# Gate and up of nine chunks a layer in seven block products where there were eight, for half of the contraction, in a two-layer decoder kernel

## The chip, the cores and the metric

The kernel runs on one core of one Trainium2 chip. The metric is the device time of one execution in microseconds (us), the median of several. The engines are TensorE (PE; its weight loads are PEld), VectorE (DVE), ScalarE (ACT), GpSimd (POOL) and the DMA queue of SyncE (SP).

## The reference

Two decoder layers on 256 tokens of width 2048, all in float32. Each layer normalises, projects, runs three causal mixers side by side and adds their output projection to the residual; all of that stays as it is. Then comes the feed-forward part, which the change touches:

```python
h2 = _rmsnorm(x, ffn_norm[l])                       # (256, 2048)
ff = jax.nn.silu(h2 @ w_gate[l]) * (h2 @ w_up[l])   # w_gate, w_up: (2048, 5632)
x = x + ff @ w_down[l]                              # w_down: (5632, 2048)
```

## The kernel before

A float32 product is made of three matmuls in a reduced float32 format: each operand is split into a rounded part (`_hi`) and a remainder (`_lo`), and hi x hi, hi x lo and lo x hi are added in PSUM. The activations `xt_hi`, `xt_lo` stay in SBUF (16 blocks of 128 rows of the contraction by 256 tokens). The weights stream in units: a unit is 4 blocks of 128 x 512 weights, 1 MB, in two transfers of 512 KB. There are four slots (`stage[s]`), taken in turn. For each unit n, SyncE waits until TensorE is done with unit n - 4 (`used[s]`), and loads it (`load`, L486); ScalarE rounds it into `w_hi[s]` (`round_unit`, L1022); VectorE writes the remainder over the staged weights as `w_lo[s]` (`rest_of_unit`, L1332); TensorE runs 24 matmuls of 512 columns on it (`unit`, L631 to L633: 4 blocks, 2 halves of the tokens, 3 matmuls) and raises `used[s]`. Each engine works strictly through its own list; ScalarE and VectorE prepare unit n + 3 (`LEAD = 3`) in the step in which TensorE runs unit n.

The hidden width 5632 is cut into 11 chunks of 512. A chunk is 8 units of gate and up (`gate_up`: 4 of gate, with the results in banks 0 and 1, then 4 of up, in banks 2 and 3) and 4 units of down (`down`, one per 512 columns of the output), where the down of chunk f - 1 follows the gate and up of chunk f. After the gate ScalarE applies Silu (L1253); after the up VectorE multiplies (L1756) into `act_sb`. In the next chunk, behind its second unit, TensorE transposes `act_sb` in eight small matmuls (`ff_turn`, L591) into banks 6 and 7; ScalarE and VectorE split that into `f_hi` and `f_lo` (L1241, L1741). Each down unit adds into `resid` with two VectorE instructions (L1765), which stand in VectorE's list ahead of the remainder of the unit prepared in the same step. The down units use banks 4/5, 0/1, 4/5, 2/3. Chunks 1 to 9 are a loop on every engine (`Fori(1, FF_CHUNKS - 1)`), one turn of it being 12 units; chunk 0 stands before the loop, chunk 10 (the peel) and the last down after it. `made(quad, n)` counts how often a slot has been filled; `x_added` counts the adds into the residual, and `added(f, n)` waits for the n-th of the down of chunk f.

Of the kernel before, what the change touches and what calls it, by code (L numbers as in the profile page):

```python
# [28 lines left out]
P = 128  # L29
# [40 lines left out]
U_BODY = U_FF + 8  # L70
U_PEEL = U_BODY + BODY * (FF_CHUNKS - 2)
# [125 lines left out]
def bank_rounds():  # L197

    used = {b: 0 for b in (4, 5, 6, 7)}
    of = {}  # L200

    def take(layer, key, banks):
        of[layer, key] = {}
        for b in banks:
            of[layer, key][b] = used[b]
            used[b] += 1

    for layer in range(DEPTH):
# [8 lines left out]
        take(layer, ("ff_turn", 0), [6, 7])  # L217
        for b in (6, 7):
            used[b] += FF_CHUNKS - 1
    return of  # L220
# [37 lines left out]
ACT_LINKS, VEC_LINKS = 9, 65  # L258

LAST_ORDER = [[(t, c) for c in range(4) for t in range(NT)], [(t, c) for t in range(NT) for c in range(4)]]  # L260
LAST_BANK = [{(t, c): (2 * (2, 0, 1, 2)[c] + t, *((-1, 6), (-1, 4), (-1, 8), (0, 2))[c]) for c in range(4) for t in range(NT)},
             {(0, 0): (4, -1, 6), (0, 1): (5, -1, 6), (0, 2): (0, -1, 6), (0, 3): (1, -1, 6),
              (1, 0): (2, -1, 8), (1, 1): (3, -1, 8), (1, 2): (0, 0, 3), (1, 3): (1, 0, 4)}]
# [5 lines left out]
def program(nc, x, positions, w_in, w_q_b, w_kv_b, w_out, w_gate, w_up, w_down, gate_w, gains, rows,  # L269
            final_norm, consts, levels, causal, out):  # L270
    with ExitStack() as ctx:
# [57 lines left out]
        stage_x = arena("stage_x", [P, 4 * NCH], F32, 32 * SEQ)  # L329
        w_lo_x = arena("w_lo_x", [P, 4 * NCH], F32R, 32 * SEQ)  # L330
        w_hi_x = arena("w_hi_x", [P, 4 * NCH], F32R, 40 * SEQ)
# [79 lines left out]
        silu_made, act_made, ft_hi_made = sem("silu_made"), sem("act_made"), sem("ft_hi_made")  # L411
# [28 lines left out]
        def made(quad, n):  # L440

            return quad + 1 - (n % 4 < 2)

# [15 lines left out]
        def _(sp):  # L459
# [33 lines left out]
            for layer in range(DEPTH):  # L493
# [45 lines left out]

                load_gate_up(U_FF, 0, 0)  # L540
                with sp.Fori(1, FF_CHUNKS - 1) as f:
                    load_gate_up(U_BODY, 3 * f - 3, f)
                    load_down(U_BODY + 8, 3 * f - 3, f - 1)
                load_gate_up(U_PEEL, 0, FF_CHUNKS - 1)
# [21 lines left out]
        def _(pe):  # L566
# [4 lines left out]
            for layer in range(DEPTH):  # L571
# [67 lines left out]
                def acc_taken(parity, r):  # L639


                    if r == 0:

                        if layer:
                            need(x_added, X_ADDS, NT * (2 + parity))
                        return
# [266 lines left out]
                def ff_turn(f):  # L913

                    pe.wait_ge(act_made, layer * (FF_CHUNKS * NT) + NT * f + NT)
                    for b in (6, 7):
                        pe.wait_ge(bank_free[b], ROUND[layer, ("ff_turn", 0)][b] + f + 1)
                        for i in range(2):
                            for t in range(NT):
                                j = 2 * (b - 6) + i  # L920
                                mm = transpose(bank[b][:, i * SEQ + t * P:i * SEQ + (t + 1) * P],
                                               act_sb[:, t, j * P:(j + 1) * P])
                        mm.then_inc(bank_full[b], 1)
# [5 lines left out]
                def gate_up(f, n0, turn=0):  # L929
                    for half in range(2):  # L930
                        if n0 == U_FF:
                            acc_taken(half, R_FF)
                        else:
                            pe.wait_ge((silu_made, act_made)[half], layer * (FF_CHUNKS * NT) + NT * f)
                            added(f - 2, 4 + 4 * half)
                        for u in range(4):
                            unit(n0 + 4 * half + u, range(4 * u, 4 * u + 4), half, normed, u == 0, u == 3,
                                 turn=turn, norm="norm2" if n0 == U_FF and half == 0 else None)
                            if n0 == U_FF and half == 0 and u == 0:
                                norm_turn("norm2", range(KT // 4, KT // 2))  # L940
                            if half == 0 and u == 1 and n0 != U_FF:
                                ff_turn(f - 1)

                def down(f, c, n0, turn=0):


                    if c == 0:
                        for b in (6, 7):
                            pe.wait_ge(bank_free[b], ROUND[layer, ("ff_turn", 0)][b] + f + 2)
                        added(f - 1, 6)  # L950
                    elif c == 2:
                        added(f, 2)
                    else:
                        pe.wait_ge(silu_made if c == 1 else act_made, layer * (FF_CHUNKS * NT) + NT * (f + 2))

                    def hidden(k):
                        return f_hi[0], f_lo[0], k

                    unit(n0 + c, range(4), (2, 0, 2, 1)[c], hidden, True, True, turn=turn)

                def last_down(f):


                    for b in (6, 7):
                        pe.wait_ge(bank_free[b], ROUND[layer, ("ff_turn", 0)][b] + f + 2)
                    last = layer == DEPTH - 1
                    for t, c in LAST_ORDER[last]:
# [10 lines left out]
                        acc = bank[b][:, :]  # L978
                        wh = hi[:, :].rearrange("p (k n) -> p k n", n=NCH)
                        wl = lo[:, :].rearrange("p (k n) -> p k n", n=NCH)  # L980
                        for k in range(4):
                            a, b = (x[1][:, k, t * P:(t + 1) * P] for x in (f_hi, f_lo))
                            pe.matmul(acc, a, wh[:, k, :], start=k == 0, stop=False)  # L983
                            pe.matmul(acc, a, wl[:, k, :], start=False, stop=False)  # L984
                            mm = pe.matmul(acc, b, wh[:, k, :], start=False, stop=k == 3)  # L985
                        mm.then_inc(used[s] if t else down_made, 1)
                        if not last and t == 1 and c >= 2:
                            norm_turn("norm1", range(2 * c - 4, 2 * c - 2), layer + 1)

                gate_up(0, U_FF)  # L990
                with pe.Fori(1, FF_CHUNKS - 1) as f:
                    gate_up(f, U_BODY, 3 * f - 3)
                    for c in range(4):
                        down(f - 1, c, U_BODY + 8, 3 * f - 3)
                gate_up(FF_CHUNKS - 1, U_PEEL)
                for c in range(4):
                    down(FF_CHUNKS - 2, c, U_PEEL + 8)
                    if c == 1:
                        ff_turn(FF_CHUNKS - 1)
# [3 lines left out]
        def _(act):  # L1003
# [26 lines left out]
            for layer in range(DEPTH):  # L1030
# [206 lines left out]
                def ff_turn(f, to):  # L1237
                    for b in (6, 7):
                        act.wait_ge(bank_full[b], ROUND[layer, ("ff_turn", 0)][b] + f + 1)
                        dst = f_hi[to][:, 2 * (b - 6):2 * (b - 6) + 2, :].rearrange("p a b -> p (a b)")  # L1240
                        act.activation(dst, bank[b][:, :], ACT.Copy).then_inc(ft_hi_made, 1)  # L1241

                def gate_up(f, n0, turn=0):
                    for i in range(8):
                        round_unit(layer * QUADS + (n0 + i + LEAD) // 4 + turn, n0 + i + LEAD)
                        if i == 1 and n0 != U_FF:
                            ff_turn(f - 1, 0)
                        if i == 3:
                            if n0 == U_FF:
                                need(rstd_made, len(POW), POW["norm2"] + 1)  # L1250
                            act.wait_ge(used[3], layer * QUADS + (n0 + 3) // 4 + 2 + turn)
# [5 lines left out]
                with act.Fori(1, FF_CHUNKS - 1) as f:  # L1257
                    gate_up(f, U_BODY, 3 * f - 3)
                    for c in range(4):
                        n = U_BODY + 8 + c + LEAD  # L1260
                        round_unit(layer * QUADS + n // 4 + 3 * f - 3, n)
                gate_up(FF_CHUNKS - 1, U_PEEL)
                for c in range(4):
                    n = U_PEEL + 8 + c + LEAD
# [3 lines left out]
                    round_unit(layer * QUADS + n // 4, n)  # L1268
                    if c == 1:
                        ff_turn(FF_CHUNKS - 1, 1)  # L1270
# [53 lines left out]
        def _(vec):  # L1324
# [22 lines left out]
            for layer in range(DEPTH):  # L1347
# [388 lines left out]
                def ff_turn(f, to):  # L1736
                    for b in (6, 7):
                        vec.wait_ge(bank_full[b], ROUND[layer, ("ff_turn", 0)][b] + f + 1)
                        vec.wait_ge(ft_hi_made, layer * (2 * FF_CHUNKS) + 2 * f + b - 5)
                        at = slice(2 * (b - 6), 2 * (b - 6) + 2)  # L1740
                        vec.tensor_tensor(f_lo[to][:, at, :].rearrange("p a b -> p (a b)"), bank[b][:, :],  # L1741
                                          f_hi[to][:, at, :].rearrange("p a b -> p (a b)").bitcast(F32), ALU.subtract)\
                           .then_inc(bank_free[b], 1)

                def gate_up(f, n0, turn=0):
                    for i in range(8):
                        rest_of_unit(layer * QUADS + (n0 + i + LEAD) // 4 + turn, n0 + i + LEAD)
                        if i == 1 and n0 != U_FF:
                            ff_turn(f - 1, 0)
                        if i == 7:  # L1750
                            if n0 == U_FF:
                                need(rstd_made, len(POW), POW["norm2"] + 1)
                            vec.wait_ge(used[3], layer * QUADS + (n0 + 7) // 4 + 2 + turn)
# [6 lines left out]
                def down(c, n0, turn=0):  # L1760
                    n = n0 + c
                    vec.wait_ge(used[n % 4], layer * QUADS + n // 4 + 2 + turn)
                    for t in range(NT):
                        part = resid[:, t, c * NCH:(c + 1) * NCH]
                        vec.tensor_tensor(part, bank[2 * (2, 0, 2, 1)[c] + t][:, :], part, ALU.add).then_inc(x_added, 1)  # L1765
                    if n == U_PEEL + 9 and layer == DEPTH - 1:
                        vec.wait_ge(hi_made_x, 1)
                        vec.tensor_tensor(w_lo_x[:, :], stage_x[:, :], w_hi_x[:, :].bitcast(F32), ALU.subtract)\
                           .then_inc(lo_made_x, 1)
                    rest_of_unit(layer * QUADS + (n + LEAD) // 4 + turn, n + LEAD)  # L1770
# [42 lines left out]
                with vec.Fori(1, FF_CHUNKS - 1) as f:  # L1813
                    gate_up(f, U_BODY, 3 * f - 3)
                    for c in range(4):
                        down(c, U_BODY + 8, 3 * f - 3)
                gate_up(FF_CHUNKS - 1, U_PEEL)
                for c in range(4):
                    down(c, U_PEEL + 8)
                    if c == 1:  # L1820
                        ff_turn(FF_CHUNKS - 1, 1)
# [58 lines left out]
```

## Time and profile before

| | |
|---|---|
| median of 3 runs | 2231.94 us (2230.34 to 2232.48) |
| the profiled execution | 2232.38 us |
| its span, first to last instruction | 2230.6 us |
| PE busy | 2212.5 us (99%), 11060 matmuls |
| PEld busy | 1889.3 us (85%) |
| DVE busy | 1277.2 us (57%) |
| ACT busy | 948.6 us (43%) |
| mean granted TensorE clock | 0.998 |
| moved by DMA | 402.67 MB, mean 181 GB/s |

Busy time is the time in which an engine has an instruction in work; matmuls are pipelined, so two of them overlap in the record (each 0.39 us long, one starting every 0.227 us), and their busy time is counted once. The chain that ended last is followed back from the last instruction, at each step to what released it.

### The profile page before, as it was taken

Reading aid. Unit: us, or ns where it says so; the run is one execution under the profiler, and the core shown is the slowest. Engines: PE = TensorE matmul, PEld = TensorE weight load, DVE = VectorE, ACT = ScalarE, POOL = GpSimd, SP = SyncE. Lnnn points to the kernel's source line nnn. Section 1 sums busy time; section 2 is a strip of 40 time slices with the busy share of each in tenths; the row PEclk is TensorE's granted clock in tenths of the full one; section 3 lists DMA queues with packets and bytes.
Section 4 is the critical chain, followed back from the end, with each engine's and each line's share of the span. In section 5 each row is a group of like instructions: output and inputs, shape, how many; then the busy total and the mean of one; then the engine's idle time right before and its main releaser. Section 6 shows DMA issues by size and latency. Waiting matters only on the chain.

```text
span 2230.6 us, 27421 instructions
## 1 busy us (share of the span) xinstructions
PE 2212.5 (99%) x11060; PEld 1889.3 (85%) x11060; DVE 1277.2 (57%) x1372; ACT 948.6 (43%) x964; POOL 24.0 (1%) x24
## 2 busy tenths in 40 slices
PE   9999999999999999999999999999999999999998
PEld 7899988888888888888888999888888888888886
DVE  5576774555455555555655866745555455555555
ACT  5554544533333333333443635444333333333333
POOL 0000000000000000000000000000000000000000
PEclk9999999999999999999999999999999999999999
DMA  7543455555555555555555435555555555555554
GB/s 249 183 134 117 157 170 189 182 191 192 189 188 188 188 190 190 192 190 192 193 179 160 147 114 166 174 171 189 197 190 192 190 189 188 188 190 189 192 191 160
DMA packets 221094, 402.67 MB, mean 181 GB/s; under 512 B 13376, under 2 KB 53600, under 8 KB 220896
## 3 DMA queue, kind: packets, MB, share of 16 engines
q1 hardware_dynamic: 220304, 400.90, 54.9%
q8 instruction: 50, 0.82, 0.1%
q10 hardware_dynamic: 720, 0.78, 0.1%
q14 instruction: 20, 0.16, 0.0%
HBM read 399.54 MB, written 2.10 MB: 180 GB/s over the span
## 4 chain that ended last, share of the span: by engine, by line
PE 97%; DMA 1%; DVE 1%; issue 1%; ACT 0%; SPq 0%; POOLq 0%; POOL 0%; ACTq 0%; DVEq 0%
PE bank L631 29%; PE bank L633 29%; PE bank L632 29%; PE bank L591 2%; DMA stage<-in_w_in 1%; PE bank L756 1%; PE bank L985 0%; PE bank L983 0%; PE bank L984 0%; PE bank L697 0%; PE bank L820 0%; PE bank L808 0%; PE bank L698 0%; PE bank L699 0%; PE bank L707 0%
## 5 line engine op out<-in xcount | busy, mean ns | idle before, releaser
L1332 DVE TENSOR_TENSOR w_lo<-stage,w_hi 128x2048 fp32r<-128x2048 f32 (+4 forms) x397 | 859.3, 2166 | 710.5 <-ACT w_hi L1022 710.4
L1022 ACT ACTIVATE w_hi<-stage 128x2048 fp32r<-128x2048 f32 (+4 forms) x397 | 719.8, 1815 | 957.7 <-DMA stage<-in_w_down 308.7
L631 PE MATMUL bank<-w_hi,xt_hi 128*128 128x512 f32 (+4 forms) x2328 | 876.6, 377 | 6.4 <-DVE xt_lo L1393 4.3
L633 PE MATMUL bank<-w_hi,xt_lo 128*128 128x512 f32 (+4 forms) x2328 | 867.7, 373 | 0.0
L632 PE MATMUL bank<-w_lo,xt_hi 128*128 128x512 f32 (+4 forms) x2328 | 867.0, 372 | 0.0
L631 PEld LDWEIGHTS bank<-w_hi,xt_hi 128*128 128x128 f32 x2328 | 437.7, 188 | 80.0 <-issue 11.8
L633 PEld LDWEIGHTS bank<-w_hi,xt_lo 128*128 128x128 f32 x2328 | 437.5, 188 | 69.0
L632 PEld LDWEIGHTS bank<-w_lo,xt_hi 128*128 128x128 f32 x2328 | 437.9, 188 | 67.8
L631 PE MATMUL bank<-w_hi,f_hi 128*128 128x512 f32 x640 | 249.1, 389 | 0.0
L633 PE MATMUL bank<-w_hi,f_lo 128*128 128x512 f32 x640 | 249.0, 389 | 0.0
L632 PE MATMUL bank<-w_lo,f_hi 128*128 128x512 f32 x640 | 249.0, 389 | 0.0
L1765 DVE TENSOR_TENSOR resid<-bank,resid 128x512 f32<-128x512 f32 x160 | 103.0, 685 | 82.1 <-PE bank L633 81.8
L633 PEld LDWEIGHTS bank<-w_hi,f_lo 128*128 128x128 f32 x640 | 120.1, 188 | 24.9
L632 PEld LDWEIGHTS bank<-w_lo,f_hi 128*128 128x128 f32 x640 | 120.1, 188 | 24.9
L631 PEld LDWEIGHTS bank<-w_hi,f_hi 128*128 128x128 f32 x640 | 120.1, 188 | 24.9
L631 PE MATMUL bank<-w_hi,mix_hi 128*128 128x512 f32 x96 | 38.5, 402 | 0.0
L633 PE MATMUL bank<-w_hi,mix_lo 128*128 128x512 f32 x96 | 37.9, 395 | 0.0
L632 PE MATMUL bank<-w_lo,mix_hi 128*128 128x512 f32 x96 | 37.9, 394 | 0.0
L1200 ACT ACTIVATE e<-e,nmx 128x128 f32<-128x128 f32 x72 | 31.8, 446 | 13.3 <-DVE nmx L1633 13.3
L1067 ACT ACTIVATE xt_hi<-bank,gain_sb 128x256 fp32r<-128x256 f32 x64 | 24.9, 480 | 24.3 <-PE bank L591 23.6
L1393 DVE SCALAR_TENSOR_TENSOR xt_lo<-bank,gain_sb,xt_hi 128x256 fp32r<-128x256 f32 x64 | 26.4, 476 | 14.2 <-ACT xt_hi L1067 13.9
L1206 ACT ACTIVATE pt<-bank 128x384 f32<-128x384 f32 x24 | 11.8, 490 | 50.6 <-PE bank L591 50.6
(213 smaller groups left out, 1231.9 us busy)
## 6 DMA issues: line engine op xcount, KB each, us to landing
stage<-in_w_gate SPq DMA_DIRECT2D x176, 512.0 KB, 4.3
stage<-in_w_up SPq DMA_DIRECT2D x176, 512.0 KB, 4.4
stage<-in_w_down SPq DMA_DIRECT2D x174, 512.0 KB, 4.4
stage<-in_w_in SPq DMA_DIRECT2D x96, 384.0 KB, 3.7
stage<-in_w_out SPq DMA_DIRECT2D x64, 512.0 KB, 4.4
stage<-in_w_in SPq DMA_DIRECT2D x54, 512.0 KB, 4.6
stage<-in_w_in SPq DMA_DIRECT2D x16, 320.0 KB, 3.4
stage<-in_w_q_b SPq DMA_DIRECT2D x12, 384.0 KB, 3.6
```

What stands on the lines that cost most here:

```text
L591: return pe.transpose(dst, src, ident)
L631: pe.matmul(acc, a, wh[:, i, :], start=first and i == 0, stop=False)
L632: pe.matmul(acc, a, wl[:, i, :], start=False, stop=False)
L633: mm = pe.matmul(acc, b, wh[:, i, :], start=False, stop=last and i == len(kts) - 1)
L756: done[par] = pe.matmul(dst, k[rows_, g, t * P:(t + 1) * P], moving, start=True, stop=True)
L1022: act.activation(w_hi[s][:, 0:kts * cols], stage[s][:, 0:kts * cols], ACT.Copy).then_inc(hi_made[s], 1)
L1067: act.activation(xt_hi[:, kt, :], bank[b][:, i * SEQ:(i + 1) * SEQ], ACT.Copy, scale=gain_sb[:, at, g0 + kt:g0 + kt + 1]).then_inc(xt_hi_m ...
L1200: last = act.activation(part, part, ACT.Exp, bias=nmx[:, k:k + 1], scale=scale, accum_out=esum[:, k:k + 1])
L1206: act.activation(pt[PT_OF[j]][:, :], ps[:, 0:3 * P], ACT.Copy).then_inc(bank_free[4], 1)
L1332: vec.tensor_tensor(w_lo[s][:, 0:kts * cols], stage[s][:, 0:kts * cols], w_hi[s][:, 0:kts * cols].bitcast(F32), ALU.subtract).then_inc(lo_ ...
L1393: ins = vec.scalar_tensor_tensor(xt_lo[:, kt, :], bank[b][:, i * SEQ:(i + 1) * SEQ], gain_sb[:, at, g0 + kt:g0 + kt + 1], xt_hi[:, kt, :]. ...
L1765: vec.tensor_tensor(part, bank[2 * (2, 0, 2, 1)[c] + t][:, :], part, ALU.add).then_inc(x_added, 1)
```

## The change

Chunks 0 and 1 of a layer stay as they were. For chunks 2 to 10 the first 8 of the 16 blocks of the contraction are computed as 2 x 2 block products in the manner of Strassen and Winograd: the two halves of the tokens by two halves of these 8 blocks, times two halves of the contraction by gate and up. Four set units (the even ones of a chunk's eight) hold one block of each of the four kinds: two of gate, two of up. TensorE makes 7 products of such a unit (`set_unit`), each into a bank of its own, where a unit had 8. The four odd units (`pair_unit`) hold two blocks of gate and two of up of the other half of the contraction, 8 products as before. What the seven products need is made as follows.

- Of the weights, VectorE makes four sums per set unit (three instructions; the second sum is written over the unit's last block) ahead of the remainders, and ScalarE rounds them: three blocks at once, then, when the sums are there, the fourth and the three others.
- Of the activations, `mixed_tokens` makes four mixed blocks once a layer, in chunk 0.
- The seven results are brought together by `combine` (four VectorE adds behind U+6, with one copy by ScalarE) and `activate` (four VectorE adds behind U+7, then the multiplications, with the Silus on ScalarE in between).

With all eight banks taken by a set chunk, the banks of down become 4/6, 5/7, 4/6, 5/7, the transposes of chunk f go behind the down of chunk f - 1, and in VectorE's list the adds into the residual move one step later, behind the preparation of the unit of the step before. The diff, cut to its core:

```diff
+SET_CHUNKS = FF_CHUNKS - FIRST_SET          # FIRST_SET = 2
+DOWN_BANKS = (4, 6), (5, 7), (4, 6), (5, 7)
+TURN_BANKS = (4, 6), (0, 1)
...
+        def in_set(n):
+            return U_BODY <= n < U_LAST and (n - U_BODY) % BODY < 8 and n % 2 == 0
...  # TensorE
+                def set_unit(n, q, f, turn):
+                    s = n % 4
+                    pe.wait_ge(lo_made[s], made(layer * QUADS + n // 4, n) + turn)
...
+                    if q == 0:
+                        pe.wait_ge(act_made, layer * (FF_CHUNKS * NT) + NT * f)
+                        pe.wait_ge(xs_made, layer + 1)
+                    product(0, token(0, q), raw[0], q == 0, False)
+                    product(1, mixed_x[3], raw[2], q == 0, False)
+                    product(2, token(1, q), summed[2], q == 0, False)
+                    if q == 0:
+                        added(f - 2, 8)
+                    product(7, mixed_x[0], summed[1], q == 0, q == 3)
+                    product(5, mixed_x[2], summed[0], q == 0, q == 3)
+                    if q == 0:
+                        hidden_in(f - 1)
+                    product(4, token(0, q + 4), raw[1], q == 0, q == 3)
+                    product(6, mixed_x[1], raw[3], q == 0, q == 3).then_inc(used[s], 1)
...
+                def down(f, c, n0, turn=0, after_set=True):
                     if c == 0:
+                        hidden_in(f)
+                        if after_set:
+                            pe.wait_ge(first_kept, layer * SET_CHUNKS + f + 2 - FIRST_SET)
+                            pe.wait_ge(combined, layer * (2 * SET_CHUNKS) + 2 * (f + 1 - FIRST_SET) + 1)
+                    elif c == 1:
+                        if after_set:
+                            pe.wait_ge(combined, layer * (2 * SET_CHUNKS) + 2 * (f + 1 - FIRST_SET) + 2)
                     else:
+                        added(f, 2 * c - 2)
...
+                with pe.Fori(FIRST_SET, FF_CHUNKS - 1) as f:
+                    gate_up_sets(f, U_BODY, 3 * f - 3 * FIRST_SET)
+                    for c in range(4):
+                        down(f - 1, c, U_BODY + 8, 3 * f - 3 * FIRST_SET)
+                    added(f - 1, 6)
+                    ff_turn(f, TURN_BANKS[0])
...  # ScalarE, prepare(n) of a set unit
+                    act.wait_ge(full[s], made(quad, n) * 32)
+                    act.activation(w_hi[s][:, 0:3 * NCH], stage[s][:, 0:3 * NCH], ACT.Copy).then_inc(raw_hi_made, 1)
+                    if between:
+                        between()
+                    act.wait_ge(sums_made, layer * (4 * SET_CHUNKS) + set_index(n) + 1 + sets)
+                    act.activation(w_hi[s][:, 3 * NCH:], stage[s][:, 3 * NCH:], ACT.Copy)
+                    act.activation(sums_hi[s // 2][:, :, :], sums[s // 2][:, :, :], ACT.Copy).then_inc(hi_made[s], 1)
...  # VectorE, prepare(n) of a set unit
+                    vec.wait_ge(full[s], made(quad, n) * 32)
+                    vec.tensor_tensor(x[:, 0:2, :], w[:, 1:3, :], w[:, 3:4, :].to_broadcast([P, 2, NCH]), ALU.add)\
+                       .then_inc(sum_chain, 1)
+                    vec.wait_ge(sum_chain, 2 * k + 1)
+                    vec.tensor_tensor(w[:, 3, :], x[:, 0, :], w[:, 2, :], ALU.add).then_inc(sum_chain, 1)
+                    vec.wait_ge(sum_chain, 2 * k + 2)
+                    vec.tensor_tensor(x[:, 2, :], w[:, 3, :], w[:, 0, :], ALU.add).then_inc(sums_made, 1)
+                    if between:
+                        between()
...
+                    vec.tensor_tensor(w_lo[s][:, 0:3 * NCH], stage[s][:, 0:3 * NCH], w_hi[s][:, 0:3 * NCH].bitcast(F32),
+                                      ALU.subtract)
+                    vec.wait_ge(hi_made[s], made(quad, n))
+                    vec.tensor_tensor(w_lo[s][:, 3 * NCH:], stage[s][:, 3 * NCH:], w_hi[s][:, 3 * NCH:].bitcast(F32),
+                                      ALU.subtract)
+                    vec.tensor_tensor(sums_lo[s // 2][:, :, :], x[:, :, :], sums_hi[s // 2][:, :, :].bitcast(F32),
+                                      ALU.subtract).then_inc(lo_made[s], 1)
...
+                def down(f, n0, turn=0, sets=0, after_set=True):
+                    def between():
+                        add_down(3, n0, turn)
+                        ff_turn(f + 1, TURN_BANKS[0], 0)
+                    for c in range(4):
+                        if c == 0 and after_set:
+                            activate(f + 1, n0 - 8, turn)
+                        if c:
+                            add_down(c - 1, n0, turn)
+                        prepare(n0 + c + LEAD, turn, sets, between if c == 3 else None)
```

## Rows read from the trace of the kernel before

**Rows 1.** The page: busy time of each engine, and the chain that ended last, by engine.

```profile
PE 2212.5 (99%) x11060; PEld 1889.3 (85%) x11060; DVE 1277.2 (57%) x1372; ACT 948.6 (43%) x964; POOL 24.0 (1%) x24
...
PE 97%; DMA 1%; DVE 1%; issue 1%; ACT 0%; SPq 0%; POOLq 0%; POOL 0%; ACTq 0%; DVEq 0%
```

**Rows 2.** One loop turn: the window's row; then a piece of the chain (start, us, what).

```profile
607.99:674.16 66.17, 66.17 (x297) 54.86 (x296) 35.09 (x24) 25.13 (x16) 0.00 (x0) 1.00 0.57 190
...
641.28 0.88 PE bank L591 x8
```

**Rows 3.** Timeline of PE at U+8: start, us, engine, line, what.

```profile
608.24 0.39 PE L633 MATMUL bank<-w_hi,xt_lo 128*128 128x512 f32 x1
...
608.92 0.39 PE L633 MATMUL bank<-w_hi,f_lo 128*128 128x512 f32 x1
```

**Rows 4.** Timeline: a unit's last matmul and its slot's next rounding (middle: U+7, ended 608.63).

```profile
481.30 0.39 PE L633 MATMUL bank<-w_hi,f_lo 128*128 128x512 f32 x1
...
487.57 1.92 ACT L1022 ACTIVATE w_hi<-stage 128x2048 fp32r<-128x2048 f32 x1 [3.91 <-DMA stage<-in_w_gate]
...
613.92 1.92 ACT L1022 ACTIVATE w_hi<-stage 128x2048 fp32r<-128x2048 f32 x1 [3.37 <-DMA stage<-in_w_down]
...
707.09 0.39 PE L633 MATMUL bank<-w_hi,xt_lo 128*128 128x512 f32 x1
...
712.46 1.92 ACT L1022 ACTIVATE w_hi<-stage 128x2048 fp32r<-128x2048 f32 x1 [2.43 <-DMA stage<-in_w_up]
```

**Rows 5.** VectorE by shape, whole span: what, xcount | busy us, mean ns | idle before.

```profile
L1332 DVE TENSOR_TENSOR w_lo<-stage,w_hi 128x2048 fp32r<-128x2048 f32 x321 | 735.3, 2292 | 661.2 <-ACT w_hi L1022 661.2
L1765 DVE TENSOR_TENSOR resid<-bank,resid 128x512 f32<-128x512 f32 x160 | 103.0, 685 | 82.1 <-PE bank L633 81.8
L1332 DVE TENSOR_TENSOR w_lo<-stage,w_hi 128x1536 fp32r<-128x1536 f32 x54 | 94.7, 1753 | 28.2 <-ACT w_hi L1022 28.2
L1756 DVE SCALAR_TENSOR_TENSOR act_sb<-bank,rstd_x,act_sb 128x512 f32<-128x512 f32 x44 | 30.9, 743 | 0.0
...
L1332 DVE TENSOR_TENSOR w_lo<-stage,w_hi 128x1024 fp32r<-128x1024 f32 x6 | 7.3, 1222 | 2.8 <-ACT w_hi L1022 2.7
```

**Rows 6.** ScalarE by shape, whole span.

```profile
L1022 ACT ACTIVATE w_hi<-stage 128x2048 fp32r<-128x2048 f32 x321 | 615.0, 1917 | 943.9 <-DMA stage<-in_w_down 308.7 <-DMA stage<-in_w_gate 288.6 <-DMA stage<-in_w_up 266.2
L1022 ACT ACTIVATE w_hi<-stage 128x1536 fp32r<-128x1536 f32 x54 | 79.8, 1478 | 2.4 <-DMA stage<-in_w_in 2.2
L1253 ACT ACTIVATE act_sb<-bank,rstd_x 128x512 f32<-128x512 f32 x44 | 27.4, 674 | 0.0
...
L1028 ACT ACTIVATE w_hi<-stage 128x512 fp32r<-128x512 f32 x4 | 2.4, 634 | 3.5 <-DMA stage<-in_w_in 3.5
```

**Rows 7.** Timeline of VectorE from the remainder prepared at U+7 to the adds of c0.

```profile
610.58 2.29 DVE L1332 TENSOR_TENSOR w_lo<-stage,w_hi 128x2048 fp32r<-128x2048 f32 x1 [3.37 <-ACT w_hi L1022]
612.79 1.40 DVE L1756 SCALAR_TENSOR_TENSOR act_sb<-bank,rstd_x,act_sb 128x512 f32<-128x512 f32 x2
614.11 1.28 DVE L1765 TENSOR_TENSOR resid<-bank,resid 128x512 f32<-128x512 f32 x2
```

**Rows 8.** Chain at a restart of TensorE, in layer 1's projection.

```profile
1210.05 1.93 ACT w_hi L1022
...
1212.00 2.30 DVE w_lo L1332
1214.30 0.14 issue
1214.43 0.36 PE bank L631
```

**Rows 9.** Start of the kernel: first matmul after a pause; the window behind it.

```profile
17.74 0.77 PE L631 MATMUL bank<-w_hi,xt_hi 128*128 128x512 f32 x1 [2.95 <-DVE xt_lo L1393]
...
17.70:20.40 2.70, 2.66 (x6) 2.15 (x7) 1.90 (x3) 2.61 (x5) 0.00 (x0) 0.50 1.05 387
```

**Rows 10.** VectorE instruction that waits for its own last result.

```profile
L1586 DVE TENSOR_TENSOR p<-p,row_sb 128x512 f32<-128x512 f32 x4 | 2.8, 692 | 0.1
```

More of the change, by code:

```diff
@@ L941, in gate_up @@
                             if half == 0 and u == 1 and n0 != U_FF:
-                                ff_turn(f - 1)
-                def down(f, c, n0, turn=0):
-                    if c == 0:
[L948 to L952, printed above, removed]
-                    else:
[L954 to L959, printed above, removed]
+                                ff_turn(f - 1, TURN_BANKS[0])
@@ new lines, in pair_unit @@
+                def pair_unit(n, m, turn):
+                    s = n % 4
+                    pe.wait_ge(lo_made[s], made(layer * QUADS + n // 4, n) + turn)
+                    for i in range(2):
+                        for t in range(NT):
+                            for part in range(2):
+                                b = 2 * part + i
+                                mm = product(2 * t + part, token(t, 8 + 2 * m + i),
+                                             (blocks(w_hi[s])[:, b, :], blocks(w_lo[s])[:, b, :]),
+                                             2 * t + part == 3 and m + i == 0, m == 3 and i == 1)
+                    mm.then_inc(used[s], 1)
@@ L1734, in _, with ff_turn @@
                 norm2()
[L1736 to L1740, printed above, removed]
+                def ff_turn(f, banks, to):
+                    for half, b in enumerate(banks):
+                        vec.wait_ge(turned, layer * (2 * FF_CHUNKS) + 2 * f + half + 1)
+                        vec.wait_ge(ft_hi_made, layer * (2 * FF_CHUNKS) + 2 * f + half + 1)
+                        at = slice(2 * half, 2 * half + 2)
@@ L1764, in down @@
                         part = resid[:, t, c * NCH:(c + 1) * NCH]
[L1765 to L1770, printed above, removed]
+                        vec.tensor_tensor(part, bank[DOWN_BANKS[c][t]][:, :], part, ALU.add).then_inc(x_added, 1)
+                def down(f, n0, turn=0, sets=0, after_set=True):
+                    def between():
+                        add_down(3, n0, turn)
+                        ff_turn(f + 1, TURN_BANKS[0], 0)
+                    for c in range(4):
+                        if c == 0 and after_set:
+                            activate(f + 1, n0 - 8, turn)
+                        if c:
+                            add_down(c - 1, n0, turn)
+                        prepare(n0 + c + LEAD, turn, sets, between if c == 3 else None)
                 def add_last(t, c):
@@ L1812, in _ @@
                 gate_up(0, U_FF)
[L1813 to L1817, printed above, removed]
-                for c in range(4):
-                    down(c, U_PEEL + 8)
-                    if c == 1:
-                        ff_turn(FF_CHUNKS - 1, 1)
+                gate_up(1, U_SECOND)
+                down(0, U_SECOND + 8, after_set=False)
+                with vec.Fori(FIRST_SET, FF_CHUNKS - 1) as f:
+                    gate_up_sets(f, U_BODY, 3 * f - 3 * FIRST_SET, 4 * f - 4 * FIRST_SET)
+                    down(f - 1, U_BODY + 8, 3 * f - 3 * FIRST_SET, 4 * f - 4 * FIRST_SET)
+                gate_up_sets(FF_CHUNKS - 1, U_PEEL)
+                for c in range(4):
+                    if c == 0:
+                        activate(FF_CHUNKS - 1, U_PEEL, 0)
+                    else:
+                        add_down(c - 1, U_PEEL + 8)
+                    if c == 1 and layer == DEPTH - 1:
+                        vec.wait_ge(hi_made_x, 1)
+                        vec.tensor_tensor(w_lo_x[:, :], stage_x[:, :], w_hi_x[:, :].bitcast(F32), ALU.subtract)\
+                           .then_inc(lo_made_x, 1)
+                    if c == 2:
+                        ff_turn(FF_CHUNKS - 1, TURN_BANKS[1], 1)
+                    prepare(U_PEEL + 8 + c + LEAD)
+                add_down(3, U_PEEL + 8)
+                vec.wait_ge(x_added, layer * X_ADDS + X_ADDS)
                 assert count[0] == VEC_LINKS, count[0]
```

254 lines of the change are left out of this document (191 added, 63 removed).

## The prediction, made before the change was run

> **What bounds the kernel now.** The busy line comes first: TensorE 99%, VectorE 57% of the span. The chain that ended last says the same from the other side, 97% of it TensorE [rows 1]. The time is thus matmuls times their spacing, and everything else counts only where TensorE comes to wait. Next, one turn of the feed-forward loop by window and by chain: 66.17 us, TensorE busy for all of it, at the full granted clock, VectorE for 35.09 us, ScalarE for 25.13 us, and eight transposes of 0.88 us [rows 2]. Last, single instructions: three matmuls start every 0.68 us, so one product (three matmuls of 512 columns) is 0.68 us and a unit of eight products 5.44 us [rows 3]. Twelve units are 65.28 us, and with the transposes 66.16: there is no wait in a turn.
>
> **What goes.** A chunk's gate and up have 64 products before. After, four set units have 7 each and four pair units 8 each: 60. So 4 x 0.68 = 2.72 us go per set chunk, with nine set chunks a layer and two layers 18 x 2.72 = 49.0 us. Every matmul keeps its form (128x128 against 512 columns), so I keep its spacing. Bytes and DMA sizes are as before: a unit is still two transfers of 512 KB, in rows of 512 numbers.
>
> **What comes, by engine.** A set unit costs VectorE one add of 1024 columns, two of 512, then remainders of 1536, 512 and 1536: 1.222 + 2 x 0.685 + 2 x 1.753 + 0.685 = 6.78 us, less about 0.2 where one starts before the last has ended, where it was 2.29 [rows 5]. Per chunk VectorE has 4 x 6.6 (sets) + 8 x 2.29 (pair and down units) + four adds of combining, four of activating, eight into the residual and two remainders of the turn, 18 x 0.64, and two multiplications, 1.4: 58 us. ScalarE has 4 x (1.478 + 0.634 + 1.478) + 8 x 1.917 + about 3.5 = 33 us [rows 6]. The new turn has 63.4 us of TensorE. No engine is over its share, but VectorE goes from 53% to 91% of a turn, in strict order, and so its order has to be walked.
>
> **The walk.** Let U be a chunk's first unit, c0 to c3 its four down units, and t = 0 the end of U+7, just before c0. I use: an end counts when the record has it, 0.16 us after the next matmul could start (0.39 long, 0.227 apart [rows 3]); the data of a slot are there 5.25 us after the end of the unit that used it, a case near the middle is 5.29, the shortest found 4.98, the longest 5.88 [rows 4]; VectorE's next instruction starts 0.09 us before the last ends where nothing holds it [rows 7] and 0.02 behind it where it needs its result [rows 10]; another engine's result is taken up 0.02 to 0.04 us later [rows 8], and TensorE's first matmul starts 0.13 us behind what it waited for [rows 8].
>
> 1. U+6 ends at -5.44. Its slot takes U+10 (c2), whose data are there at -0.2. VectorE is in the remainder of U+9 until -0.7, then starts combining; the first difference, which frees banks 4 and 6, is ready at -0.14. c0 starts at 0.0 in place of -0.16: wait 0.16 us.
> 2. Combining ends at 1.75, the remainder of U+10 at 4.03. Only then comes `activate`, behind it in order: four adds, 3.94 to 6.4; ScalarE's two Silus run 4.7 to 5.9, and the two multiplications end at 7.8.
> 3. U+11 (c3): data at 5.25, ScalarE, held by the Silus, 5.84 to 7.76; remainder 7.79 to 10.08.
> 4. Only now the adds of c0 (c0 had ended at 5.60): to 11.27. c2 uses c0's banks and could start at 10.88, starts at 11.40: wait 0.52 us.
> 5. U+12, the next chunk's first set unit: data at 5.60 + 5.25 = 10.85. Sums 11.18 to 13.84; ScalarE's second part 13.88 to 15.90; VectorE's first remainder to 15.63, then it stands for ScalarE, then 15.93 to 18.28.
> 6. Only now the adds of c1 (c1 had ended at 11.04): 18.19 to 19.46. c3 uses banks 5 and 7, as c1 did, and waits for just these (`added(f, 4)`). c2's last matmul has made room at 16.84; c3 starts at 19.59: wait 2.75 us.
> 7. Behind it: remainder of U+13 to 21.7, adds of c2 to 22.9, sums of U+14 to 25.4, adds of c3 to 26.6, remainders of the turn to 28.1. TensorE ends c3 at 25.0, turns until 25.9, and reaches the wait for c3's adds at 27.9 and that for the turn's remainders at 29.3: 1.2 us to spare at both. U+14 is ready at 31.9 and wanted at 36.1, and inside the eight units the slack only grows.
>
> So a loop turn waits 0.16 + 0.52 + 2.75 = 3.43 us and saves 2.72: 63.44 + 3.43 = 66.87 us where it was 66.17. The kernel before had the same adds, but ahead of the remainder in each step and beside ordinary remainders of 2.29 us: there each step's adds follow their unit's end at once [rows 7].
>
> **Sum.** Per layer, nine set chunks save 24.5. Eight loop turns wait 27.4; the down of chunk 0, before the loop, already prepares U+12 as a set unit, but has no `activate`: 0.07 + 2.85 = 2.9; the last chunk's down prepares ordinary units: only the 0.16 ahead of c0. Together 30.5: a layer is 6.0 us longer, two 12.1. Arrival is not even, and only late data add to the wait while early ones are cut short by other waits: I add 1. The mixed tokens, in chunk 0, are one operation of 2048, four of 512 and one of 2048, 7.3 us a layer; units there have 3.1 us of VectorE idle each, and 6.8 us between being ready and being wanted, of which 5 are used by the longest piece: nothing. Without this cover they would cost 7 a layer. The tail behind the last down is unchanged. The profiled execution took 2232.4 (span 2230.6), so 2245.5; the median is 0.4 less: 2245.
>
> **Bounds of what no row shows.** Each of these moves the wait before c3 one for one, so 18 times. The 1024 add takes one of its sources by broadcast: as a 512 one or as a 1536 one, 0.69 or 1.75 in place of 1.22, so -10 or +10 us; I take 1.22, the width that it writes [rows 5]. Arrival: 5.0 to 5.9 against 5.25, -4 or +12. A wait on its own result: 0.0 to 0.1 us, two per chain: up to +3. A start without the overlap of 0.09, where the many waits between VectorE's instructions would break it: some ten of them from `activate` to c1's adds, not all on the chain: up to +20. TensorE's restart, 0.13 us in its one row: 0 to 0.3, -2 or +3. The forecast's own range is 2229 to 2262.
>
> **Rivals.**
> (a) *The clock falls in the wait.* After 2.95 us without a matmul at the start of the kernel the granted clock was 0.50, that is 1.2 of 2.4 GHz, for 2.7 us, six matmuls 0.45 us apart in place of 0.227: 1.34 us lost [rows 9]. The wait before c3 is 2.75 to 2.9 us, nearly as long. If each of the 18 does this: 24 us more, 2269. Against it: this wait is a little shorter, and it is the only such row. The Trainium skill, "TensorE: Matmul & The Clock Gate", section "Why this matters for your kernels", asks for no idle stretches between bursts of matmuls, as one lets the engine fall to half rate; the trace agrees once, at 2.95 us, and no row of this case has a wait of 2.75.
> (b) *The wait isn't there* (the other side). It needs the adds of c1 to be done by 16.7, that is 2.75 us of step 2 to 6 to be gone: VectorE would take c1's adds ahead of the remainders of U+12, or TensorE's wait would be met by earlier adds. By the written order neither is so: for c2 and c3 `added(f, 2 * c - 2)` asks for 2 and 4, and `add_down(1)` stands behind `prepare` of U+12. If only the short waits stay: 49.0 - 18 x 0.68 = 37 gained, 2195. It decides from the point at which the chain from c0's end to c1's adds is under 11.1 us; I have 13.9.
> (c) *VectorE is the bound throughout.* Its 52 instructions a chunk carry more waits than before. With 0.1 us more on each, 5.2 us a turn, half of it lies on the path: about +33 over the forecast, 2278. For it: 91% busy already in the sum. Against: waits between engines cost 0.02 to 0.04 us in every row of before.
> (d) *A shorter chain*: same waits, but each link at its low bound (-14 in all): 2231, no change.
>
> **Chances.** Forecast 0.58, (a) 0.15, (b) 0.12, (c) 0.06, (d) 0.09. Within 0.2% of the time before (about what a measurement here can tell from no change) is 2227.5 to 2236.4. Faster: (b), and a part of (d): 0.16. Same: the rest of (d) and the low end of the forecast: 0.14. Slower: 0.70. The range 2226 to 2270 leaves out (b) and (c).
>
> **What would show it.** In the profile after, one loop turn lasts 66.9 us and its TensorE is busy for some 63.4. The longest wait of TensorE is by the adds into the residual, once a turn, 2.7 us, 18 in all (nine a layer); behind it 0.5 us by the same line, and 0.16 by combining. VectorE's last remainder of U+12 ends right before the adds of c1. No wait inside the eight gate and up units. A granted clock below 1.00 in the loop, with matmuls 0.45 us apart behind the long wait, speaks for (a); loop turns of 63.4 to 64.2 us for (b); waits of TensorE for weight remainders for (c). I would be wrong altogether if a matmul's spacing were to change, or if waits stood inside gate and up.

## The result, and the profile after

The changed kernel takes 2268.81 us (median of 4, 2266.61 to 2272.14) where the kernel before takes 2231.26: a ratio of 1.0169, 95% interval 1.0152 to 1.0187. It is slower, as forecast (2245), and by 37.5 us in place of 13 to 14. The number is that of rival (a), 2269, in which the clock falls in the wait before c3.

The page of the changed kernel, against [rows 1]: VectorE went from 1277 to 1684 us, TensorE from 11060 to 10844 matmuls, that is 18 x 12 fewer, and the chain that ended last is no longer TensorE almost alone.

```profile
PE 2195.1 (97%) x10844; PEld 1856.5 (82%) x10844; DVE 1684.0 (74%) x1888; ACT 1076.8 (48%) x1128; POOL 24.0 (1%) x24
...
PE 75%; DVE 10%; issue 6%; DMA 5%; ACT 3%; SPq 1%; DVEq 0%; POOLq 0%; POOL 0%; ACTq 0%
```

The waits of TensorE (engine, line waited for: us, times, longest): one pair of lines that the kernel before doesn't have leads, matmuls of down behind the adds into the residual.

```profile
PE bank L994 <- DVE resid L1997: 50.8, 34, 2.9
```

Two loop turns by window (us, PE busy, PEld, DVE, ACT, POOL, granted clock, DMA share, GB/s), each from the start of one c3 to the next, against the 66.17 us of [rows 2]. The second is 1.57 us longer and its clock lower; the two last windows show where: the first 3.66 us of each turn hold 16 matmuls in the first and 9 in the second, at a mean granted clock of 0.56.

```profile
630.42:697.57 67.15, 64.30 (x284) 52.39 (x284) 56.97 (x53) 32.05 (x25) 0.00 (x0) 1.00 0.57 188
697.57:766.29 68.72, 65.86 (x284) 53.54 (x284) 57.07 (x53) 32.04 (x25) 0.00 (x0) 0.98 0.56 182
697.57:701.23 3.66, 3.66 (x9) 2.84 (x10) 3.66 (x4) 0.69 (x1) 0.00 (x0) 0.56 0.60 229
630.42:634.08 3.66, 3.66 (x16) 3.04 (x17) 3.66 (x4) 0.84 (x1) 0.00 (x0) 1.00 0.60 231
```

The timeline of TensorE at the start of the second window (start, us, engine, line, what). c3's first matmul starts 2.79 us behind the start of the one before it, where 0.227 is the usual spacing [rows 3], so it is 2.57 us late. From 698.25 on matmuls start 0.43 us apart, as at 1.2 GHz (half clock, in what follows), and the spacing comes back behind 701.57.

```profile
694.78 0.39 PE L996 MATMUL bank<-w_hi,f_lo 128*128 128x512 f32 x1
697.57 0.50 PE L994 MATMUL bank<-w_hi,f_hi 128*128 128x512 f32 x1 [2.40 <-DVE resid L1997]
697.91 0.53 PE L995 MATMUL bank<-w_lo,f_hi 128*128 128x512 f32 x1
698.25 0.63 PE L996 MATMUL bank<-w_hi,f_lo 128*128 128x512 f32 x1
698.67 0.63 PE L994 MATMUL bank<-w_hi,f_hi 128*128 128x512 f32 x1
...
701.23 0.49 PE L994 MATMUL bank<-w_hi,f_hi 128*128 128x512 f32 x1
701.57 0.40 PE L995 MATMUL bank<-w_lo,f_hi 128*128 128x512 f32 x1
```

All 18 waits before c3 are there: 16 of 2.56 to 2.58 us, and the first of each layer with 3.02 and 2.81. Behind 11 of the 18 six to eight matmuls follow 0.43 us apart; the longest wait, 3.02 us, is not among the 11.

VectorE's own timeline, up to the c3 at 630.42, can be laid beside the walk of the prediction. Its t = 0, the end of U+7, is 610.64 here. The walk had the sums of U+12 from 11.18, the last remainder to 18.28, c1's adds from 18.19 and c3 at 19.59; the rows have 11.42, 18.52, 18.44 and (630.42) 19.78.

```profile
614.72 0.68 DVE L1976 TENSOR_TENSOR kept<-bank,kept 128x512 f32<-128x512 f32 x1
...
618.66 2.28 DVE L1481 TENSOR_TENSOR w_lo<-stage,w_hi 128x2048 fp32r<-128x2048 f32 x1
620.86 1.28 DVE L1997 TENSOR_TENSOR resid<-bank,resid 128x512 f32<-128x512 f32 x2
622.06 1.21 DVE L1905 TENSOR_TENSOR sums<-stage 128x1024 f32<-128x1024 f32 x1
623.30 0.69 DVE L1908 TENSOR_TENSOR stage<-sums,stage 128x512 f32<-128x512 f32 x1
624.03 0.69 DVE L1910 TENSOR_TENSOR sums<-stage 128x512 f32<-128x512 f32 x1
624.75 1.76 DVE L1915 TENSOR_TENSOR w_lo<-stage,w_hi 128x1536 fp32r<-128x1536 f32 x1
626.80 0.69 DVE L1918 TENSOR_TENSOR w_lo<-stage,w_hi 128x512 fp32r<-128x512 f32 x1 [0.29 <-ACT sums_hi L1365]
627.41 1.75 DVE L1920 TENSOR_TENSOR sums_lo<-sums,sums_hi 128x1536 fp32r<-128x1536 f32 x1
629.08 1.28 DVE L1997 TENSOR_TENSOR resid<-bank,resid 128x512 f32<-128x512 f32 x2
```

### The profile page after: what moved, and what is told of

The parts are those of the page before. It is cut to its first block, busy times and chain, and to the rows that moved or that the text cites. A ratio compares the mean times of both kernels' runs of the same rounds, so it can differ in the third digit from the quotient of the medians.

```text
span 2264.8 us, 27939 instructions
## 1 busy us (share of the span) xinstructions
PE 2195.1 (97%) x10844; PEld 1856.5 (82%) x10844; DVE 1684.0 (74%) x1888; ACT 1076.8 (48%) x1128; POOL 24.0 (1%) x24
## 4 chain that ended last, share of the span: by engine, by line
PE 75%; DVE 10%; issue 6%; DMA 5%; ACT 3%; SPq 1%; DVEq 0%; POOLq 0%; POOL 0%; ACTq 0%
PE bank L994 12%; PE bank L996 11%; PE bank L995 11%; PE bank L673 11%; PE bank L675 11%; PE bank L674 11%; DMA stage<-in_w_down 3%; PE bank L633 2%; ACT w_hi L1130 2%; DVE resid L1997 1%; DVE sums_lo L1920 1%; ACT sums_hi L1365 1%; DVE sums L1905 1%; DMA stage<-in_w_in 1%; DVE w_lo L1481 1%
## 5 line engine op out<-in xcount | busy, mean ns | idle before, releaser
L1481 DVE TENSOR_TENSOR w_lo<-stage,w_hi 128x2048 fp32r<-128x2048 f32 (+3 forms) x325 | 693.8, 2137 | 350.2 <-ACT w_hi L1130 348.8
L1130 ACT ACTIVATE w_hi<-stage 128x2048 fp32r<-128x2048 f32 (+3 forms) x325 | 581.4, 1791 | 434.4 <-DMA stage<-in_w_down 207.5
L673 PE MATMUL bank<-w_hi,xt_hi 128*128 128x512 f32 (+4 forms) x1176 | 426.0, 362 | 4.3 <-DVE xt_lo L1542 3.1
L675 PE MATMUL bank<-w_hi,xt_lo 128*128 128x512 f32 (+4 forms) x1176 | 418.8, 356 | 0.0
L674 PE MATMUL bank<-w_lo,xt_hi 128*128 128x512 f32 (+4 forms) x1176 | 418.4, 356 | 0.0
L994 PE MATMUL bank<-w_hi,xt_hi 128*128 128x512 f32 x720 | 281.6, 391 | 0.0
L996 PE MATMUL bank<-w_hi,xt_lo 128*128 128x512 f32 x720 | 280.2, 389 | 0.0
L995 PE MATMUL bank<-w_lo,xt_hi 128*128 128x512 f32 x720 | 280.1, 389 | 0.0
L1360 ACT ACTIVATE w_hi<-stage 128x1536 fp32r<-128x1536 f32 x72 | 107.3, 1491 | 249.9 <-DMA stage<-in_w_up 249.9
L1915 DVE TENSOR_TENSOR w_lo<-stage,w_hi 128x1536 fp32r<-128x1536 f32 x72 | 126.4, 1755 | 1.8
```

The costliest lines, as they stand in the source:

```text
L673: pe.matmul(acc, a, wh[:, i, :], start=first and i == 0, stop=False)
L674: pe.matmul(acc, a, wl[:, i, :], start=False, stop=False)
L675: mm = pe.matmul(acc, b, wh[:, i, :], start=False, stop=last and i == len(kts) - 1)
L994: pe.matmul(bank[b][:, :], x[0], w[0], start=start, stop=False)
L995: pe.matmul(bank[b][:, :], x[0], w[1], start=False, stop=False)
L996: return pe.matmul(bank[b][:, :], x[1], w[0], start=False, stop=stop)
```

## The experiments

The theory: the order of VectorE's list makes the waits, above all the one before c3, and TensorE's standing still there brings the half clock. Against it stand VectorE's load (57 of 67 us a turn), and a cause of the half clock other than the wait.

**1. c1's adds before the remainders of U+12.** In VectorE's `down`:

```diff
-                        if c:
+                        if c in (1, 3):
                             add_down(c - 1, n0, turn)
-                        prepare(n0 + c + LEAD, turn, sets, between if c == 3 else None)
+                        prepare(n0 + c + LEAD, turn, sets,
+                                {1: lambda: add_down(1, n0, turn), 3: between}.get(c))
```

> The changed kernel with one thing moved in VectorE's list: the adds of c1 into the residual stand between the sums and the remainders of U+12 instead of behind them. Theory (the order of VectorE's list makes the long wait, and the wait makes the clock fall): the wait before c3 (2.57 us a turn) is gone, c2's of about 0.6 us and the 0.2 us before c0 stay, no matmul in the loop runs 0.43 us apart; 18 x 2.6 us of waiting and some 11 x 1.6 us of half clock go from 2268.8: 2203 us. Rival (VectorE's load of 85% is what holds TensorE): the wait moves to another place, remainders of the weights among them, and the time stays above 2230 us.

Measured: 2223.15 us (2220.13 to 2223.43), ratio to the kernel before 0.9958 (0.9941 to 0.9974). The wait before c3 and every half clock of the feed-forward part are gone, the time is under 2230 as the theory has it, but 20 us over its number. The trace of this kernel says where they went: TensorE, earlier now, runs into the wait for c3's adds at the fourth product of the next chunk.

```profile
633.92 0.39 PE L996 MATMUL bank<-sums_hi,xt_lo 128*128 128x512 f32 x1
635.03 0.50 PE L994 MATMUL bank<-sums_hi,xs_hi 128*128 128x512 f32 x1 [0.72 <-DVE resid L1997]
```

It comes 0.88 us late there, and 0.70 to 1.05 us in all 18 places, 14.3 us together; with the slower restart behind each (see below) that is some 16 of the 20 us. The reason stands in VectorE's list of the same kernel: the adds of c3 wait behind the sums of U+14.

```profile
629.74 1.29 DVE L1997 TENSOR_TENSOR resid<-bank,resid 128x512 f32<-128x512 f32 x2
631.11 1.23 DVE L1905 TENSOR_TENSOR sums<-stage 128x1024 f32<-128x1024 f32 x1
632.37 0.69 DVE L1908 TENSOR_TENSOR stage<-sums,stage 128x512 f32<-128x512 f32 x1
633.09 0.69 DVE L1910 TENSOR_TENSOR sums<-stage 128x512 f32<-128x512 f32 x1
633.70 1.28 DVE L1997 TENSOR_TENSOR resid<-bank,resid 128x512 f32<-128x512 f32 x2
```

The 1.2 us to spare of the walk's step 7 were 1.2 us behind a wait of 2.75; take the wait away, and TensorE reaches the wait for c3's adds before they are done. I had not carried that into the expectation.

**2. c0's adds ahead of the remainder of U+11 too.** As in 1, with `if c in (0, 3): add_down(c and c - 1, n0, turn)`.

> As the one before, and the adds of c0 stand ahead of the remainder of U+11 as well, in the step of c0. Theory: the wait of 0.6 us before c2 goes too, with its restart; only the 0.2 us before c0 stays: 2203 - 18 x 0.65 = 2191 us, under both the kernel before and the changed one. Rival (VectorE's load): U+11 or U+12 comes late instead, TensorE waits for a remainder before c3 or before the next chunk, and nothing is gained over the kernel with only c1's adds moved (2203 us).

Measured: 2218.26 us (2217.80 to 2219.81), ratio 0.9942 (0.9925 to 0.9958). c2's wait went, and 5 us with it, not 12: the rest came back as waits before the transposes, which ask for c2's adds. The waits of TensorE in this kernel:

```profile
PE bank L633 <- DVE resid L1997: 11.9, 18, 1.0
PE bank L994 <- DVE resid L1997: 9.9, 18, 0.6
```

Neither the theory's 2191 nor the rival's sign: no wait for a remainder of the loop's weights leads here, all are for adds. So the question was whether the order alone could take the rest away, or whether VectorE was short of time by now; experiment 6 is for that.

**3. The wait filled.** Nothing moved; ahead of the wait for c1's adds TensorE gets ten matmuls (2.43 us in the record) whose results are used by nothing.

```diff
+                    if c == 3 and n0 != U_PEEL + 8:
+                        pe.wait_ge(act_made, layer * (FF_CHUNKS * NT) + NT * (f + 1) + NT)
+                        for _ in range(10):
+                            pe.matmul(bank[0][:, :], f_hi[0][:, 0, 0:P], blocks(w_hi[s])[:, 0, :], start=True, stop=True)
+                    if c >= 2:
+                        added(f, 2 * c - 2)
```

> The changed kernel with nothing moved; TensorE gets ten matmuls of 512 columns more ahead of the wait before c3, into bank 0, which is free then and is written afresh by the next unit; their result is used by nothing. Theory (the clock falls because TensorE stands still for 2.57 us): the ten matmuls, 2.27 us, lie in the wait, a turn without half clock stays at 67.2 us, and no turn has half clock any more: 2268.8 - 11 or 12 x 1.6 = 2250 us, although there are 180 matmuls more. Rival (the half clock has another cause, or the added time is not the clock's): the time stays at 2269 us or rises by what the ten matmuls add.

Measured: 2249.50 us (2249.27 to 2249.82), ratio 1.0081 (1.0064 to 1.0098): 19.3 us less than the changed kernel (0.88% by the two ratios, 19.6), with 180 matmuls more. No matmul of the feed-forward part runs 0.43 us apart any more, and every loop turn is 67.1 to 67.3 us. The timeline of this kernel at one c3: the ten matmuls stand where TensorE stood still, the first matmul of c3 comes 2.88 us behind the last one of c2 (2.79 in the changed kernel's rows), and full speed follows.

```profile
626.84 0.39 PE L996 MATMUL bank<-w_hi,f_lo 128*128 128x512 f32 x1
627.07 2.43 PE L1062 MATMUL bank<-w_hi,f_hi 128*128 128x512 f32 x10
629.72 0.50 PE L994 MATMUL bank<-w_hi,f_hi 128*128 128x512 f32 x1 [0.22 <-DVE resid L2001]
630.05 0.40 PE L995 MATMUL bank<-w_lo,f_hi 128*128 128x512 f32 x1
630.29 0.39 PE L996 MATMUL bank<-w_hi,f_lo 128*128 128x512 f32 x1
```

So half of what the changed kernel loses, 19 of 37.5 us, is half clock, and it comes from TensorE's standing still. The two profiled executions, 2266.61 and 2249.27 us, differ by 17.3 us, which is the 11 occurrences counted there at 1.57 us each.

**4, 5, 7 and 9. Other lengths of standing.** Four kernels ask how long TensorE has to stand. In 4, c1's adds stand ahead of only the last remainder of U+12; 7 is 4 with two VectorE adds into free scratch tiles ahead of them; 5 is the changed kernel with one such add; 9 is experiment 3 with four matmuls for ten.

```diff
+                        if c == 2:                     # 5
+                            vec.tensor_tensor(kept[1][:, :], resid[:, 0, 0:NCH], resid[:, 1, 0:NCH], ALU.add)
...
+                    for i in range(2):                 # 7, ahead of add_down(1)
+                        vec.tensor_tensor(kept[i][:, :], resid[:, 0, 0:NCH], resid[:, 1, 0:NCH], ALU.add)
...
-                        for _ in range(10):            # 9, against 3
+                        for _ in range(4):
```

> The changed kernel with the adds of c1 moved ahead of only the last remainder of U+12 (1536 columns, 1.66 us in the list). The wait before c3 becomes about 1.0 us in all 18 places. Theory (a wait this short leaves the clock): no half clock, 2268.8 - 18 x 1.66 - 11 x 1.6 = 2221 us. Rival (any wait lets the clock fall in the same share of cases): half clock behind some 11 of the 18 waits still, 2239 us.

> The changed kernel with one VectorE add of 512 columns more (into a scratch tile that is free there, its result is used by nothing) ahead of the adds of c1: the wait before c3 grows by 0.6 us, from 2.57 to about 3.2 us, 18 times. Theory (the longer TensorE stands, the surer half clock follows): it follows all 18 waits in place of 11, so 2268.8 + 18 x 0.6 + 7 x 1.6 = 2291 us, granted clock below 0.989. Rival (the share has nothing to do with the length of the wait): 11 of 18 still, 2280 us.

> The kernel with the shorter wait (0.9 us before c3, 2229.9 us) with two more adds of 512 columns on VectorE into free scratch tiles ahead of the adds of c1: a wait before c3 of about 2.1 us. If half clock comes only behind waits near 2.6 us and above, there is none: 2229.9 + 18 x 1.2 = 2251 us. If a wait of 2.1 us is long enough for some of the 18 to be followed by it, as at 2.57 us, it is up to 2251 + 11 x 1.6 = 2269 us, and the granted clock says which.

> The changed kernel with four matmuls of 512 columns more, in place of ten, ahead of the wait before c3, into a bank that is free there; their result is used by nothing. TensorE stands for about 1.7 us there instead of 2.57 us, while everything else, and the length of a turn, stays. No half clock followed 0.9 us, it followed 16 of 18 waits of 2.1 us and 11 of 18 of 2.57 us. If 1.7 us is short enough the time is that of ten matmuls, 2250 us, and the granted clock 0.998; if half clock still follows in most turns it is 2265 to 2275 us.

| kernel | standing before c3 | followed by half clock, of 18 | mean clock | loop turn | median us (ratio, interval) |
|---|---|---|---|---|---|
| 4 | 0.9 us | 0 | 0.998 | 66.0 | 2229.91 (0.9995; 0.9986 to 1.0005) |
| 9 | 1.7 us (one of 2.0) | 1, behind the 2.0 | 0.997 | 67.2 (one of 68.9) | 2252.31 (1.0098; 1.0081 to 1.0115) |
| 7 | 2.1 us | 16 | 0.985 | 68.3 (one of 67.1) | 2269.86 (1.0169; 1.0152 to 1.0186) |
| changed | 2.57 us | 11 | 0.989 | 67.2 or 68.8 | 2268.81 (1.0169; 1.0152 to 1.0187) |
| 5 | 3.16 us | 15, seven of them twice as long | 0.981 | 67.9 to 71.2 | 2292.37 (1.0267; 1.0250 to 1.0285) |

One c3 of experiment 7 in TensorE's timeline, and the window behind it: 1.94 us idle in the record, 2.1 us late, and a granted clock of 0.54.

```profile
702.20 0.50 PE L994 MATMUL bank<-w_hi,f_hi 128*128 128x512 f32 x1 [1.94 <-DVE resid L1999]
```

```profile
703.00:706.50 3.50, 3.50 (x10) 2.72 (x10) 3.50 (x3) 0.99 (x1) 0.00 (x0) 0.54 0.53 207
```

And one of experiment 9, 1.58 us idle, with full speed behind it:

```profile
698.98 0.50 PE L994 MATMUL bank<-w_hi,f_hi 128*128 128x512 f32 x1 [1.58 <-DVE resid L2001]
699.31 0.39 PE L995 MATMUL bank<-w_lo,f_hi 128*128 128x512 f32 x1
699.54 0.40 PE L996 MATMUL bank<-w_hi,f_lo 128*128 128x512 f32 x1
```

The count is of stretches with at least three matmuls in a row 0.41 to 0.445 us apart. The standing is that of most of the 18 places; the first one of a layer is up to 0.5 us longer. In 4 the theory was right on the clock and 9 us low on the time, 5.7 of them again by the adds of c3 (0.3 us late a turn). In 5 the time was as expected (2291), but by luck: half clock follows 15 waits and not 18, and in seven of them 12 or 13 matmuls in a row are slow and not 5 to 7 (turns of 70.5 us and more, where 67.9 has none), which makes up for the missing three. Experiment 9 met its first case, with one exception, and the exception is its longest wait, 2.0 us; none of the 17 others, 1.70 to 1.80 us, is followed by half clock, so that 1.7 us of standing costs next to nothing beyond its length.

Experiment 7 was the surprise: a *shorter* wait than the changed kernel's, and half clock behind 16 of 18. An occurrence is cheaper there, 68.33 against 67.07 us for a turn, as TensorE, late by then, no longer has the 0.3 us wait for c3's adds that the turn without half clock has. So the length is a condition (none of the 35 waits before c3 of up to 1.8 us in 4 and 9, most of those from 2.1 us), but it is not all that decides. In the changed kernel turns of 67.2 and 68.8 us follow each other in a pattern (one of the short, then two of the long), which speaks for the moment at which the wait falls; what it is measured against no run here shows, and I leave it open.

**6. All adds in the order in which TensorE asks for them.** VectorE's `down` becomes:

```diff
+                        if c != 1:
+                            add_down(c, n0, turn)
+                        if c == 3:
+                            ff_turn(f + 1, TURN_BANKS[0], 0)
+                        prepare(n0 + c + LEAD, turn, sets,
+                                (lambda: add_down(1, n0, turn)) if c == 1 else None)
```

> As the kernel with both adds moved (2218.3 us), and the rest of VectorE's list at the end of down put in the order in which TensorE wants it: the adds of c2 ahead of the remainder of U+13, the adds of c3 and the remainders of the transposes ahead of the sums of U+14. Theory (VectorE has the time, its order lacked it): the waits of 0.8 us before the transposes and of 0.7 us before the fourth product of the next chunk go, only the 0.2 us before c0 stays, a turn is 63.7 us: 2218 - 18 x 1.5 = 2191 us. Rival (VectorE's load is the bound by now): the 1.5 us of work put off comes back as waits for the remainders of U+14 to U+16, and the time stays at 2210 us or above.

Measured: 2189.51 us (2186.35 to 2190.70), ratio 0.9806 (0.9790 to 0.9822), as the theory has it. VectorE does the same work (1677.5 us) in a time 79 us shorter than the changed kernel's, and a loop turn is 63.6 to 64.0 us; one stretch of that length by window:

```profile
605.00:668.80 63.80, 63.64 (x285) 52.41 (x284) 56.53 (x53) 32.06 (x26) 0.00 (x0) 1.00 0.59 197
```

VectorE is at 89% of the turn, and TensorE waits for no weight remainder in the loop. VectorE's load as the bound is ruled out.

**8. Combining one step earlier.** As 6, with `if i == 7:` made `if i == 6:` ahead of `combine` on VectorE and ahead of ScalarE's copy of bank 4.

> The kernel with all adds moved (2189.5 us), and combining (four VectorE adds and ScalarE's copy of the first product) one step earlier, ahead of the preparation of U+9 in place of behind it. Theory: the first difference, for which c0 waits, is ready some 4 us before it is wanted; the waits before c0 go (0.2 to 0.3 us and the restart in 16 turns, 1.6 us once in the last chunk of layer 0): 2189.5 - 7 = 2182 to 2184 us. Rival (VectorE, which waits for U+6 there, holds up U+9 to U+11): waits for remainders before the down units, 2190 us or more.

Measured: 2183.31 us (2181.60 to 2185.07), ratio 0.9789 (0.9773 to 0.9805): 2.1% under the kernel before. The waits before c0 are gone; one loop turn by window has TensorE busy without a gap.

```profile
605.00:668.50 63.50, 63.50 (x286) 52.65 (x285) 56.78 (x53) 31.78 (x25) 0.00 (x0) 1.00 0.60 198
```

## Why the prediction was wrong in size

The sign, the place of the waits and what causes them held. What such a wait does to the clock behind it was missing from the forecast. **What goes** was 49.0 us, and is that: the best kernel, with the same matmuls and no waits in the loop, is some 47 us under the kernel before (ratio 0.9789), and its turn is 63.48 us in the mean against 66.19, so 2.71 us shorter, where the forecast had 2.72.

**The walk** held within 0.3 us at every step (the rows above show the later ones), and so did its waits: 2.57 for 2.75 before c3, 0.48 to 0.75 for 0.52 before c2, 0.06 to 0.27 for 0.16 before c0. Only a turn without half clock is 67.15, where the walk had 66.87. That is the restart: the second matmul behind a wait comes another 0.1 us late (629.72 to 630.05 in experiment 3's rows is 0.33 for 0.227, and the changed kernel has 0.34 at 697.57), three times a turn, 0.3 us. [Rows 8] had the first matmul's 0.13 us only, and before c3 that one is 0.06 (c1's adds end at 630.36, c3 starts at 630.42). With 18 turns the 0.28 us are 5 us.

**The step that failed** is the one that gave the wait before c3 its price: its length and nothing behind it, with the clock set aside as rival (a) at 0.15, "as it is the only such row". [Rows 9] had all of it: 2.95 us of standing, then 1.34 us lost at half clock. Here one occurrence costs 1.57 us (68.72 against 67.15), close to that row, and there are 11 in the profiled execution, 17 us; experiment 3 takes away 19.3. The sum then closes within a microsecond: 13.7 forecast over the median of before, 5 of restarts and 19.3 of half clock are 38 us, and 37.5 were measured. Rival (a) had the right total by luck, through two errors that cancel: it counted 18 occurrences at 1.34 and no restarts.

Rival (b), waits that aren't there, and (d), a shorter chain, did not come true. (c), VectorE as the bound throughout, was ruled out by experiments 6 and 8; its price was also wrong in itself, as half of 5.2 us over 18 turns is 47 us and not 33. The Trainium skill's advice in "TensorE: Matmul & The Clock Gate", section "Why this matters for your kernels", against idle stretches between bursts of matmuls was the thing to weigh more heavily; the trace agrees, with 11 of 18 stretches of 2.57 us. The section gives it for longer stretches than experiment 7's 2.1 us, and there the measurement decides.

What I said of step 7, 1.2 us to spare, was right for the changed kernel (no wait stands there) and misleading for mending it: it cost experiments 1 and 2, and in part 4, their numbers.

## What to carry to other kernels

When an edit gives an in-order engine more to do, a sum of busy times says little (89% busy can mean no wait, 85% a loss of 85 us against the best order); walk its list once against the moments at which the bounding engine asks for each result, and put short results that free a bank ahead of long preparations. A wait of the matmul engine of some 2 us or more is to be priced at its length plus the half clock that can follow it, here 1.3 to 1.6 us each and about 2.7 in the turns with 12 slow matmuls. When one wait is removed, walk the turn again before naming the gain, because slack behind it was measured from a late start.

## What the runs showed of the hardware that I had not expected

- A kernel with 180 more matmuls is 19.3 us faster (2249.5 against 2268.8 us), because they fill a wait.
- Half clock follows a shorter wait more often (16 of 18 at 2.1 us) than a longer one (11 of 18 at 2.57 us); at 1.70 to 1.80 us it followed none of 17, and at 0.9 us none of 18.
- Behind 3.16 us of standing it lasts for 5 to 7 matmuls in some turns and for 12 or 13 in others.
- The second matmul after a wait is 0.1 us late (0.33 to 0.34 us for 0.227), on top of the first one's delay, after waits of 0.06 us and of 2.57 us alike.
